# Sixteen instead of thirty-two of a gate row's adds in the attention, forty-eight in the output projection, and its last chunk token tile by token tile

## What is computed

```
mod_x = (sc_ @ w_ada[l] + b_ada[l])[:, None, :]
sh1, s1, g1, sh2, s2, g2 = jnp.split(mod_x, N_MOD, axis=-1)
...
x = x + g1 * (_merge_heads(o_da, o_mla, subln_w[l], lambda_init) @ w_o[l])
h2 = _modulate(_rmsnorm(x, norm2_w[l]), sh2, s2)
x = x + g2 * _conv_ffn(h2, w_up[l], conv_w[l], conv_b[l], w_down[l])
```

## Time and profile before

| | us |
|---|---|
| median of three runs | 2914.86 |
| profiled execution | 2916.72 |
| its span, first to last instruction | 2914.9 |
| PE busy | 2804.3 (96%) |
| DVE busy | 1766.2 (61%) |
| ACT busy | 1234.9 (42%) |

### The profile page before, as it was taken

The page is one execution under the profiler, slowest core; times in us unless marked ns, Lnnn a source line. Parts: engine busy times, 40 slices in busy tenths (PEclk is TensorE's granted clock), DMA queues, the critical chain, the costliest instruction groups (busy, mean ns, idle before and its releaser), DMA issues.

```text
span 2914.9 us, 34309 instructions
## 1 busy us (share of the span) xinstructions
PE 2804.3 (96%) x13474; PEld 2288.9 (79%) x13474; DVE 1766.2 (61%) x1959; ACT 1234.9 (42%) x1345; POOL 168.9 (6%) x340
## 2 busy tenths in 40 slices
PE   6899998899999999999999999998899999999998
PEld 2587875687888888888888888888788888888887
DVE  2586777875655555555665567975745455545554
ACT  4232216644444434435465443434644444434333
POOL 0000215100000000000000000015300000000000
PEclk9999999999999999999999999999999999999999
DMA  9798975784545565546657776666266555556554
GB/s 391 283 334 277 330 266 176 244 308 145 187 160 189 197 219 189 171 161 212 222 201 242 244 232 218 221 190 203 87 190 206 191 189 188 176 196 201 165 173 152
DMA packets 348574, 621.44 MB, mean 213 GB/s; under 512 B 49792, under 2 KB 102672, under 8 KB 340896
## 3 DMA queue, kind: packets, MB, share of 16 engines
q1 hardware_dynamic: 311568, 586.76, 60.1%
q10 hardware_dynamic: 36880, 32.94, 3.4%
HBM read 590.64 MB, written 29.00 MB: 213 GB/s over the span
## 4 chain that ended last, share of the span: by engine, by line
PE 89%; DVE 4%; ACT 2%; DMA 2%; issue 1%; SPq 0%; POOL 0%; ACTq 0%; DVEq 0%; POOLq 0%
PE ps L309 23%; PE ps L311 23%; PE ps L310 23%; PE ps L1187 3%; PE ps L1188 3%; PE ps L1189 3%; PE ps L1470 1%; PE ps L414 1%; DVE w_lo L958 1%; DMA ctx_in<-in_ctx 1%; PE ps L1857 1%; DMA raw<-in_pack_ada 1%; DVE w_lo L271 1%; PE ps L1457 0%; PE ps L2891 0%
## 5 line engine op out<-in xcount | busy, mean ns | idle before, releaser
L271 DVE TENSOR_TENSOR w_lo<-raw,w_hi 128x2048 fp32r<-128x2048 f32 (+3 forms) x428 | 894.6, 2098 | 673.6 <-ACT w_hi L264 672.3
L264 ACT ACTIVATE w_hi<-raw 128x2048 fp32r<-128x2048 f32 (+3 forms) x428 | 747.3, 1757 | 733.5 <-PE ps L311 687.6
L309 PE MATMUL ps<-w_hi,a_hi 128*128 128x512 f32 x2240 | 876.9, 391 | 3.4 <-DVE a_lo L795 2.7
L311 PE MATMUL ps<-w_hi,a_lo 128*128 128x512 f32 x2240 | 872.3, 389 | 0.0
L310 PE MATMUL ps<-w_lo,a_hi 128*128 128x512 f32 x2240 | 871.6, 389 | 0.0
L309 PEld LDWEIGHTS ps<-w_hi,a_hi 128*128 128x128 f32 x2240 | 420.5, 188 | 90.2 <-DVE a_lo L795 3.3
L311 PEld LDWEIGHTS ps<-w_hi,a_lo 128*128 128x128 f32 x2240 | 420.4, 188 | 87.8
L310 PEld LDWEIGHTS ps<-w_lo,a_hi 128*128 128x128 f32 x2240 | 420.7, 188 | 85.9
L309 PE MATMUL ps<-w_hi,b_hi 128*128 128x512 f32 x796 | 312.3, 392 | 3.7 <-DVE b_lo L834 3.7
L310 PE MATMUL ps<-w_lo,b_hi 128*128 128x512 f32 x796 | 310.2, 390 | 0.0
L311 PE MATMUL ps<-w_hi,b_lo 128*128 128x512 f32 x796 | 310.2, 390 | 0.0
(11 more groups left out here) (373 smaller groups left out, 2775.2 us busy)
## 6 DMA issues: line engine op xcount, KB each, us to landing
raw<-in_hyb_w_in SPq DMA_DIRECT2D x96, 1024.0 KB, 5.9
raw<-in_sc_w_in SPq DMA_DIRECT2D x96, 1024.0 KB, 5.1
raw<-in_w_up SPq DMA_DIRECT2D x88, 1024.0 KB, 5.0
raw<-in_pack_ada SPq DMA_DIRECT2D x96, 512.0 KB, 6.1
raw<-in_w_down SPq DMA_DIRECT2D x48, 768.0 KB, 4.4
raw<-in_w_in SPq DMA_DIRECT2D x24, 1024.0 KB, 7.6
raw<-in_hyb_w_out SPq DMA_DIRECT2D x32, 768.0 KB, 4.5
raw<-in_sc_w_out SPq DMA_DIRECT2D x32, 768.0 KB, 4.5
```

The costliest lines, as they stand in the source:

```text
L264: nc.scalar.activation(w_hi[s][:, 0:n_k, 0:ncols], raw[s][:, 0:n_k, 0:ncols], ACT.Copy).then_inc(sem("hi_done"), 1)
L271: nc.vector.tensor_tensor(w_lo[s][:, 0:n_k, 0:ncols], raw[s][:, 0:n_k, 0:ncols], w_hi[s][:, 0:n_k, 0:ncols].bitcast(F32), ALU.subtract).th ...
L309: nc.tensor.matmul(o, h, w_hi[s][:, k, 0:ncols], start=kt == 0, stop=False)
L311: last = nc.tensor.matmul(o, l, w_hi[s][:, k, 0:ncols], start=False, stop=kt == L.groups[-1][0] + L.groups[-1][1] - 1)
```

## The change

Four things are changed.

1. `G2_ATT` is 4 instead of 8. The first four rows are added in attention units 16 to 23, and units 24 to 31 have no adds. Rows 4 to 15 are added in the output projection, three a chunk (`G2_WO = 3`), so 48 adds instead of 32.
2. The SP stream follows. The four loads of rows 4 to 7 leave the attention. Rows 4 and 5 are loaded behind the pieces of chunk 0 into the `g2_row` buffers. The load of row 6, which waits for row 4's adds, stands at the end of n = 0. In chunks 1 to 3 a row is loaded behind each of the pieces 1, 2 and 3.
3. The last chunk runs by token tile. ACT's squares of tile 0 and DVE's residual of tile 0 stand ahead of the first pieces of `UP`.
4. `gate_out` stands behind the diagonal matrices. PE's second transposed pair, which uses the same PSUM bank (5) as `g2_total`, waits for it.

```diff
@@ -334,8 +334,8 @@
 
         def tile_done(eng, L, n, t):
 
-            if t == 0 and L is not WO:
-                eng.wait_ge(sem("tile_done"), 1 + (DOWN[1], HO, SO).index(L))
+            if t == 0:
+                eng.wait_ge(sem("tile_done"), 1 + (WO, DOWN[1], HO, SO).index(L))
             else:
                 chunk_done(eng, L, n)
 
@@ -706,6 +706,8 @@
 
             n_banks = FLIP_BANKS[name] if name in FLIP_BANKS else 2
             flip = nc.tensor.transpose if name != "n2" else (lambda o, x, r: nc.tensor.matmul(o, x, r, start=True, stop=True))
+            if name == "n2" and j == 1:
+                pe.wait_ge(sem("gate_row"), 2)
             if j >= n_banks and name in FLIP_BANKS:
                 pe.wait_ge(sem("flip_lo"), flips_before(name) + j - n_banks + 1)
             elif name == "mix2" and j == 1:
@@ -1264,7 +1266,8 @@
             sp.dma_start(v_in[h % 2][:], tok(src)).then_inc(sem(f"at_v_in{h % 2}"), 16)
 
         g2_run = put_a("g2_run", [P, D])
-        G2_ATT = KT // 2
+        G2_ATT = RING
+        G2_WO = (KT - G2_ATT) // 4
         g2_row = [place(f"g2_row{i}", [P, D], at=b) for i, b in enumerate((BH, BL))]
 
         def g2_slot(kt):
@@ -1608,7 +1611,7 @@
             dst = o_all[:, t, bass.ds(head_col(h, i, HD), HD)]
             nc.vector.tensor_scalar(dst, ps[:, 7, 0:HD], mx[t][:, 6:7], None, ALU.mult).then_inc(sem("at_o"), 1)
 
-        G2_ADDS = [0] * (2 * HEADS) + [2] * (2 * HEADS)
+        G2_ADDS = [0] * (2 * HEADS) + [2] * HEADS + [0] * HEADS
         assert sum(G2_ADDS) == ADA_COLS * G2_ATT
 
         def g2_rows(u):
@@ -1779,12 +1782,14 @@
                 gate_load(sp, n, 0, n)
                 for g, (kt, n_k) in enumerate(WO.groups if n else ()):
                     load_piece(sp, WO, WO.p0 + n * WO.per + g, kt, n_k, n * CHUNK)
-                    if g % 2:
-                        g2_load(sp, G2_ATT + 2 * n + g // 2)
+                    if g:
+                        g2_load(sp, G2_ATT + G2_WO * n + g - 1)
+                if n == 0:
+                    g2_load(sp, G2_ATT + 2)
 
         def wo_pe(pe, hooks):
             for n in range(4):
-                matmul_chunk(pe, WO, n, WO.c0 + n, [mix], hooks=hooks if n == 0 else {})
+                matmul_chunk(pe, WO, n, WO.c0 + n, [mix], hooks=hooks if n == 0 else {}, by_tile=n == 3)
             g2_total(pe)
 
         def presplit(split, eng, L, first=0, n=3, w=CHUNK):
@@ -1803,14 +1808,14 @@
 
         def wo_dve(dve, chain):
             for n in range(4):
-                def adds(first, count=2):
+                def adds(first, count=G2_WO):
                     for a in range(first, first + count):
-                        g2_add(dve, G2_ATT + 2 * n + a // ADA_COLS, a % ADA_COLS)
-
-                hooks = {1: lambda: adds(0), 2: lambda: adds(2), 3: lambda: (residual(dve, chain, WO, n - 1, n - 1), adds(4)),
-                         "end": lambda: adds(6)} if n else {
+                        g2_add(dve, G2_ATT + G2_WO * n + a // ADA_COLS, a % ADA_COLS)
+
+                hooks = {1: lambda: adds(0), 2: lambda: adds(3), 3: lambda: (residual(dve, chain, WO, n - 1, n - 1), adds(6)),
+                         "end": lambda: adds(9)} if n else {
                     "end": lambda: (flip_lo(dve, "mix", (4, 5), mix_scale, b_hi, b_lo), adds(0, 4),
-                                    flip_lo(dve, "mix", (6, 7), mix_scale, b_hi, b_lo), adds(4, 4))}
+                                    flip_lo(dve, "mix", (6, 7), mix_scale, b_hi, b_lo), adds(4, 8))}
                 split_chunk(split_lo, dve, WO, n, hooks=hooks, skip=3 if n == 0 else 0)
 
 
@@ -3450,8 +3455,9 @@
                 if g < 2:
                     flip_hi(act, "mix", (2 * g, 2 * g + 1), mix_scale, b_hi)
             wo_act(act)
+            x_squares(act, "n2", WO, 3, [0])
             presplit(split_hi, act, UP[0])
-            x_squares(act, "n2", WO, 3)
+            x_squares(act, "n2", WO, 3, [1])
             root_act(act, "n2", 2, 10)
             late_store(act, 1)
             flip_act(act, "n2", KT // 2, a_hi)
@@ -3492,13 +3498,13 @@
                 if g < 2:
                     flip_lo(dve, "mix", (2 * g, 2 * g + 1), mix_scale, b_hi, b_lo)
             wo_dve(dve, chain)
+            residual_tile(dve, chain, WO, 3, 0)
             presplit(split_lo, dve, UP[0], 0, 2)
-            residual_tile(dve, chain, WO, 3, 0)
             residual_tile(dve, chain, WO, 3, 1)
+            sum_parts(dve, "n2", 10, 8)
+            norm_diag_dve(dve, "n2", TILES, 10, chain)
             dve.wait_ge(sem("msum"), N_ADA + N_LATE + 1)
             gate_out(dve, 1, 5)
-            sum_parts(dve, "n2", 10, 8)
-            norm_diag_dve(dve, "n2", TILES, 10, chain)
             flip_dve(dve, "n2", KT // 2, c_of("m2"), c_of("sh2"), a_hi, a_lo, {4: lambda: presplit(split_lo, dve, UP[0], 2)})
             up_dve(dve, chain, 0, 3)
             down_dve(dve, chain, 0)
```

## The result

The changed kernel takes 2931.07 us, median of 4 runs (2930.8 to 2935.35), the kernel before 2914.53 in the same session (4 runs, 2911.06 to 2916.37). The ratio is 1.0058, 95% interval 1.0046 to 1.0070: slower by 16.5 us. Forecast were 2933.7 and a range of 2922 to 2940.

What follows compares the result with a forecast made beforehand. The prediction took the projection as PE-bound with 4 to 6 us of lead. Waits of +19.2, clock +1.5 and end -1.9 gave +18.8 on the median 2914.86: 2933.7 us, 80% range 2922 to 2940.

Steps and rivals of the forecast that it cites:

- Attention, 16 adds less: Attention's second half: 10.6 us of DVE work goes, all beside PE; worth 0, at best 1.0 us.
- First stall 7.0: Near piece (0,3): PE waits 7.0 us for `b_lo`, held up behind the late load of piece (1,0); at least 3.3.
- chunk 1 9.05 late: Start of projection chunk 1: after 2.05 us more waiting for `w_lo` of (1,0), at 599.1 instead of 590.1.
- The gate's load 1.2 us in the queue: Loads ahead of piece (1,0): the gate behind row 6 takes some 1.2 us, chosen between nothing and 2.6.
- Chunks 1 and 2: Projection rounds take 23.1 us against PE's 21.8; waits of 0.45, 0.2 and 1.1 bring the sum to 10.8.
- Chunk 3: By-tile last chunk: PE waits 2.6, 1.9 and 3.9 us for pieces (3,1), (3,2), (3,3), 8.4 in all.
- the clock 1.5: Behind the 3.9 us wait in chunk 3: PE at a lower granted clock costs 1.5 us, between 0 and 2.8.
- The end: Projection's last matmul to first transpose with the diagonals: 3.6 us instead of 5.5, a gain of 1.9.
- Sum: Whole kernel: +19.2 + 1.5 - 1.9 = +18.8 us, giving 2933.7 us.
- Late but not starved: Rival: chunk 3's pieces keep up with tile 0, so its 8.4 and 1.5 go; +8.9, 2923.8 us; chance 0.20.
- The round is longer: Rival: slower load queue in the projection rounds and 2.8 for the clock; +23.6, 2938.5 us; chance 0.12.
- Only the end: Rival: (1,0) not held by row 4's adds, lead covers the adds, only -1.9 remains; 2913.0 us, chance 0.08.

Runs made afterwards that it cites:

- control: The kernel before, unchanged, profiled a second time: one execution, 2909.48 us.
- e3: Changed kernel with row 6's load issued behind pieces (1,0) and (1,1) instead of ahead of them: 2923.41 us.
- e7: Changed kernel with ACT making `b_hi` of all four last columns ahead of the `w_hi` of piece (1,0): 2927.27 us.
- e4: Changed kernel with the first gate's four columns loaded once ahead of the projection, so no gate load in the rounds: 2923.01 us.
- e1: Kernel before with only the last projection chunk by token tile and the reordered end, row adds left as before: 2914.97 us.
- e2: Changed kernel with the last projection chunk and the end put back as before, only the row moves kept: 2923.54 us.
- e6: Kernel before with only the gate output row moved behind the diagonals, PE's second pair of transposes waiting for it: 2913.8 us.
- e8: Kernel before with last chunk by token tile, end reordered and first gate loaded once ahead of the projection; run twice: 2911.45 and 2912.14 us.

## Why the prediction was right, point by point

- **Attention, 16 adds less: 0.** The changed kernel was 2.85 us ahead at 495 us, ahead of the adds that were taken out, and 2.83 ahead where the projection starts. The half of the attention in question gave 0.0, and the waits for ACT's copies are 5.4 us in 7 in both kernels. The 2.8 themselves are within the control's scatter.
- **First stall 7.0, chunk 1 9.05 late.** 6.74 beyond the normal step, and 8.95. The two links were shown apart: e3 (the load alone moved: all gone) and e7 (ACT's order alone: 7.1 of the 8.95). The split by waits was a little off: I had 7.0 and then 2.05 of waiting for `w_lo` of (1,0); measured were 6.7 of waiting and then a piece that took 7.70 us instead of 5.45 at the low clock, at whose end the `w_lo` was there. The end point is the same since the `w_lo` sets it. One sum of the prediction is wrong here: 583.3, 1.2 and 2.65 make 587.15 and not 587.6. Rightly added, chunk 1 would have been forecast 8.6 late and the whole at about 18.35 us. The piece landed at 584.74, which is 587.57 counted as in the kernel before (2.83 us later), since the row and the gate took 0.4 more than was put in: that this point came out to 0.1 us is luck.
- **The gate's load 1.2 us in the queue.** The row landed after 5.1 (580.58), the gate after 6.2 (582.07): 1.5, and the piece 2.7 later (584.74). Without the gate, in e4, the piece lands 2.7 behind the row. The choice between nothing and 2.6 was near enough.
- **Chunks 1 and 2: to 10.8 at (3,0).** 9.79. A round was forecast at 23.1 us; from gate to gate it was 22.2 (606.13 to 628.30). This is the term that was most oversized, by 1.0. The walk had 5.0 for the gate of chunk 2 and 7.65 for (2,0) behind it; measured from the gate's issue at 606.13 were 3.3 and 6.9. One round later they were 5.2 and 7.9 (628.30), so why this one was quicker stays open.
- **Chunk 3: 8.4 and the clock 1.5.** The three waits: 2.30, 1.71 and 3.92 beyond the normal step, 7.9 in all (forecast 2.6, 1.9, 3.9). The clock: the last matmul is 19.82 late, so 19.82 - 9.79 - 7.93 = 2.1, 0.6 more than forecast. That the starving needs both halves is e1 and e2; that two of the three waits go with the gate's wait is e4.
- **The end: -1.9.** 9.41 against 11.31 from the last matmul to the up projection: -1.90. e6 gives 0.57 of it to the gate output row. (The prediction's 655.55 is the start of `g2_total`; the last matmul starts 0.23 us sooner.)
- **Sum: 18.8.** 9.79 + 7.93 + 2.10 - 1.90 = 17.92. The path, the places of the long waits and every sign were right. The sum is nearer than its terms because their misses (1.0 and 0.5 too much, 0.6 too little) partly cancel. The medians differ by 16.5; the 1.4 between are smaller than the scatter of the parts that the change doesn't touch.
- **Rivals.** "Late but not starved" fell by the three waits. "The round is longer" fell by the 22.2. "Only the end" fell by SP's issue at 575.82 and after. In the text of the second, a gate of 2.6 "in three rounds is 4.2 by itself" was wrongly worked out: the walk has the full 7.65 from the gate's issue to the piece in the second and third round already, so only the first could grow, by 1.4.

## What to carry to other kernels

A load that waits for a consumer holds everything issued after it on the same engine: put it behind the loads that have nothing to wait for (here one line, 9.5 us). The same holds on the engine that takes the data: work that is ready belongs in front of an operation that may wait (e7, 6.8 us). And before a loop is reordered so that it asks for its operands in a burst, look at the lead of the loads at that point: with the lead that the old order left (e1) it cost 0.6 us and gave 1.9, without it (e3) it cost 10.

## What the runs showed of the hardware that was not expected

- The same idle gap of PE is followed by the low clock in some executions and not in others: behind 1.98 us at the diagonals in the control and in e2 but not in the first profile of before; behind 1.81 us ahead of the projection in e6 but not in the other 11 profiles. The low clock costs 0.7 to 0.85 us behind the first of these and 1.6 behind the second. Behind the wait at (3,1) the granted clock was 1.00 in the changed kernel (2.14 us idle, 645 to 650) and 0.66 in e3 (2.18, 635 to 640). The Trainium skill (TensorE: Matmul & The Clock Gate, "What's actually happening") says of the slow matmuls at a kernel's start that their number varies from run to run. The trace agrees that one program isn't always granted the same clock at one place, with 0.66 and 1.00 here; this case shows it for the fall behind a wait, not for the start. An edit that takes a gap away can thus gain more than the gap in some executions; e8's medians (2.8 and 3.1 us against a stage of 1.9) may hold some of that, which isn't shown.
- A low clock in front of a wait for data costs little, because the data catches up meanwhile: piece (0,3) of the changed kernel (2.25 us longer, chunk 1 still 0.1 us from the forecast) and (3,1) of e3 (its next wait gone). Gap and clock must not be summed before asking what comes late next.
